# Layer norms taken by token halves, with ScalarE centring and scaling three of four chunks, in a fused two-layer transformer kernel

## The reference, cut to what matters

```python
def layer_norm(x, g, b):
    xf = x.astype(jnp.float32)
    mu = xf.mean(-1, keepdims=True)
    var = jnp.square(xf - mu).mean(-1, keepdims=True)
    return ((xf - mu) * lax.rsqrt(var + LN_EPS) * g.astype(jnp.float32) + b.astype(jnp.float32)).astype(x.dtype)

def swiglu(x, w_in, w_out):
    g, u = jnp.split(x @ w_in, 2, axis=-1)
    return (jax.nn.silu(g) * u) @ w_out

# first_block
y = hybrid_mixer(x, ...)
x = layer_norm(ALPHA * x + y, ln_g[l, 0], ln_b[l, 0])
y = mem_cross_attention(x, mem, w_q_mem[l], w_kv_mem[l], w_o_mem[l])
x = layer_norm(ALPHA * x + y, ln_g[l, 1], ln_b[l, 1])
y = swiglu(x, w_ffn_in[l], w_ffn_out[l])
x = layer_norm(ALPHA * x + y, ln_g[l, 2], ln_b[l, 2])

# second_block
hn = rmsnorm(x, norm_g)
proj = jnp.einsum('bsd,dc->bsc', hn, w_in)
```

## Time and profile before

| | |
|---|---|
| median of 3 runs | 2252.07 us (2250.58 to 2252.34) |
| the profiled execution | 2250.64 us, span 2248.8 us |
| TensorE busy | 2231.8 us, 99% of the span |
| VectorE, ScalarE, GpSimd busy | 58%, 46%, 8% |
| mean granted TensorE clock | 0.998 |
| chain that ended last | TensorE 96%, VectorE 2%, GpSimd 1% |
| weights and x read | 418 MB, 187 GB/s over the span |

### The profile page before, as it was taken

One profiled execution on the slowest core, in us unless ns is written; L12 is line 12 of the kernel. 1 busy time (PEld: TensorE's weight loads), 2 busy tenths in 40 slices (PEclk: granted clock), 3 DMA queues, 4 the chain that ended last, 5 costly groups with the idle time before them and its releaser, 6 DMA issues.

```text
span 2248.8 us, 29509 instructions
## 1 busy us (share of the span) xinstructions
PE 2231.8 (99%) x10256; PEld 1849.3 (82%) x10256; DVE 1307.9 (58%) x1571; ACT 1038.8 (46%) x1239; POOL 173.0 (8%) x175
## 2 busy tenths in 40 slices
PE   9999999999999999999999999999999999999999
PEld 8888888888888788888888888877888888888887
DVE  5555655566667854454445545566666656645674
ACT  4444445545444444433444344435445454445643
POOL 1000000001203210000000000003000000200020
PEclk9999999999999999999999999999999999999999
DMA  7755654556755365656655565555566665765554
GB/s 234 227 174 164 185 159 159 189 163 213 263 177 198 123 230 181 197 190 193 192 189 187 187 197 186 192 172 159 161 194 197 195 194 171 218 186 174 168 188 167
DMA packets 216454, 421.29 MB, mean 187 GB/s; under 512 B 15240, under 2 KB 19376, under 8 KB 214448
## 3 DMA queue, kind: packets, MB, share of 16 engines
q1 hardware_dynamic: 212928, 401.79, 56.5%
q0 software_dynamic: 3168, 17.82, 2.4%
q10 hardware_dynamic: 272, 0.52, 0.1%
HBM read 417.97 MB, written 2.11 MB: 187 GB/s over the span
## 4 chain that ended last, share of the span: by engine, by line
PE 96%; DVE 2%; POOL 1%; DMA 0%; ACT 0%; issue 0%; ACTq 0%; SPq 0%; DVEq 0%
PE b_ps L571 90%; PE b_ps L599 1%; PE b_ps L616 1%; PE b_ps L668 1%; DVE b_w_lo L1479 1%; PE b_ps L683 1%; POOL b_x_res L499 1%; DVE b_x_res L1630 0%; DVE b_x_res L1639 0%; PE b_ps L677 0%; PE b_ps L759 0%; PE b_ps L736 0%; POOL b_x_res L510 0%; POOL b_x_res L505 0%; PE b_ps L684 0%; DMA b_gate_a<-in_x 0%
## 5 line engine op out<-in xcount | busy, mean ns | idle before, releaser
L1479 DVE TENSOR_TENSOR b_w_lo<-b_stage,b_w_hi 128x1024 fp32r<-128x1024 f32 (+1 forms) x762 | 935.2, 1246 | 618.1 <-ACT b_w_hi L1065 615.3
L1065 ACT ACTIVATE b_w_hi<-b_stage 128x1024 fp32r<-128x1024 f32 (+1 forms) x762 | 794.5, 1054 | 685.2 <-PE b_ps L571 656.7
L571 PE MATMUL b_ps<-b_w_hi,b_x_hi 128*128 128x512 f32 (+1 forms) x2364 | 938.5, 397 | 0.7 <-DVE b_w_lo L1479 0.5
L571 PE MATMUL b_ps<-b_w_hi,b_x_lo 128*128 128x512 f32 (+1 forms) x2364 | 921.0, 390 | 0.0
L571 PE MATMUL b_ps<-b_w_lo,b_x_hi 128*128 128x512 f32 (+1 forms) x2364 | 919.4, 389 | 0.0
L571 PEld LDWEIGHTS b_ps<-b_w_hi,b_x_lo 128*128 128x128 f32 x2364 | 444.5, 188 | 93.6
L571 PEld LDWEIGHTS b_ps<-b_w_hi,b_x_hi 128*128 128x128 f32 x2364 | 445.0, 188 | 92.2 <-issue 3.2
L571 PEld LDWEIGHTS b_ps<-b_w_lo,b_x_hi 128*128 128x128 f32 x2364 | 445.2, 188 | 87.6
L571 PE MATMUL b_ps<-b_w_hi,b_ff_h 128*128 128x512 f32 x352 | 137.3, 390 | 0.0
L571 PE MATMUL b_ps<-b_w_hi,b_ff_l 128*128 128x512 f32 x352 | 137.0, 389 | 0.0
L571 PE MATMUL b_ps<-b_w_lo,b_ff_h 128*128 128x512 f32 x352 | 136.9, 389 | 0.0
(11 more groups left out here) (294 smaller groups left out, 1462.3 us busy)
## 6 DMA issues: line engine op xcount, KB each, us to landing
b_stage<-in_w_in SPq DMA_DIRECT2D x335, 512.0 KB, 4.2
b_stage<-in_w_ffn_in SPq DMA_DIRECT2D x176, 512.0 KB, 4.5
b_stage<-in_w_ffn_out SPq DMA_DIRECT2D x88, 512.0 KB, 4.1
b_stage<-in_w_out SPq DMA_DIRECT2D x64, 512.0 KB, 4.0
b_stage<-in_w_up SPq DMA_DIRECT2D x24, 512.0 KB, 4.1
b_stage<-in_w_o_dsa SPq DMA_DIRECT2D x16, 512.0 KB, 4.7
b_stage<-in_w_o_moba SPq DMA_DIRECT2D x16, 512.0 KB, 4.3
b_stage<-in_w_kv_mem SPq DMA_DIRECT2D x16, 512.0 KB, 3.5
```

Of the source, the lines that this page charges most:

```text
L571: ins = mm(ps[:, ACC + r, 0:n], x[:, kt + t, rows], w[:, slot, t, 0:n], start=first and t == 0 and k == 0, stop=last and t == GK - 1 and k ...
L1065: act.activation(w_hi[:, slot, :, 0:n], stage[:, slot, :, 0:n], ACT.Copy)\
L1479: dve.tensor_tensor(w_lo[:, slot, :, 0:n], stage[:, slot, :, 0:n], w_hi[:, slot, :, 0:n].bitcast(F32), ALU.subtract).then_inc(sem("lo_done ...
```

## The change

In norms 1 and 2 (`feed_normed`, `norm_and_feed`) the work goes by token halves. Norm 0 keeps its split of work.

- TensorE: in the last block before each of the two norms the last two groups run for half 0, then for half 1 (`two_groups`, `rows_last`). The first two groups after the norm do the same. Batches 0 and 1 are turned for half 0, then two half groups, then batches 0 and 1 for half 1, directly followed by batches 2 and 3, which go to two other PSUM banks (`SC`, `PT`), then the two other half groups. Fillers go from 19 + 15 to 3 + 6 + 3 + 4.
- VectorE does residual, statistics, aggregation, centring of all 512 columns of chunk one, root and scaling for half 0, then the residual of half 1 and the low parts of half 0, then the same for half 1. It also computes `shift` = -mean x rstd. Chunk two is no longer its work.
- ScalarE does (x - mean) x rstd for chunks two to four as x x rstd + shift. Batches 2 and 3 are turned from that; weight and bias of the norm, which then lie along partitions, are applied as it reads PSUM (`ln_gc`, `ln_bc`, result in `nat`), and high and low parts are taken from `nat`.
- GpSimd only multiplies by the weight and adds the bias (`weigh`), in chunks three, four, then two.
- Four more loads of 128 x 16 single elements bring `ln_gc` and `ln_bc`; for norm 2 GpSimd multiplies them once by `g_col`.
- In norm 0 GpSimd's multiply and add alternate by half, each waiting for the one before.

The core of the diff:

```diff
-LN_FILL = (19, 15)
+LN_FILL = (3, 6, 3, 4, 5)
@@ GpSimd
+            for m in (1, 2):
+                load(ln_gc[:, m - 1, :], a["ln_g"][m, :].rearrange("(t p) -> p t", p=P), "small2",
+                     allow_slow_non_contiguous=True)
+                load(ln_bc[:, m - 1, :], a["ln_b"][m, :].rearrange("(t p) -> p t", p=P), "small2",
+                     allow_slow_non_contiguous=True)
...
+                    for n in (2, 3):
+                        for r in range(R):
+                            pool.wait_ge(sem("scaled"), 5 * m - 5 + (1, 3, 4, 5)[2 * (n - 2) + r])
+                            ins = weigh(n, r)
+                        ins.then_inc(sem("late_chunk"), 1)
+                    pool.wait_ge(sem("tp_done"), c.at(f"turned{m}"))
                     for r in range(R):
...
+                        ins = weigh(1, r)
@@ TensorE
+            def two_groups(kt, first, last, hi, lo, ready=None):
+
+                slot = c.value("g") % SLOTS
+                for r in range(R):
+                    for i in range(2):
+                        if ready:
+                            ready(r, i)
+                        if r == 0:
+                            pe.wait_ge(sem("lo_done"), c.next("lo_done"))
+                        half_group((slot + i) % SLOTS, r, kt + i * GK, first and i == 0, last and i == 1, hi, lo)
+                c.next("g", 2)
...
+                def rows_ready(r, i):
+                    if i == 0:
+                        keep_warm(LN_FILL[2 * r])
+                        for t in range(2):
+                            pe.wait_ge(sem("chunk"), 4 * m + 2 * r + t)
+                            turn_rows(t, r).then_inc(sem("tp_done"), 1)
+                        c.next("tp_free", 2)
+                        if r == 1:
+                            pe.wait_ge(sem("scaled"), 5 * m - 3)
+                            for t in (2, 3):
+                                for row in range(R):
+                                    ins = turn_rows(t, row)
+                                ins.then_inc(sem("tp_done"), 1)
+                            c.next("tp_free", 2)
+                        keep_warm(LN_FILL[2 * r + 1])
+                    pe.wait_ge(sem("tp_free"), fed + 2 * r + i + 1)
+                two_groups(0, True, False, x_hi, x_lo, ready=rows_ready)
+                for j in range(2, KT // GK):
+                    pe.wait_ge(sem("tp_free"), fed + 4 + j - 1)
+                    group(j * GK, False, j == KT // GK - 1, x_hi, x_lo)
+                    if j + 2 < KT // GK:
+                        if j % 2 == 0:
+                            pe.wait_ge(sem("late_chunk"), 3 * m - 1 + j // 2)
+                        feed_batch(x_res, j + 2)
@@ ScalarE
+                for r in range(R):
+                    root(sd[:, r:r + 1])
+                    if r == 1:
+                        scaled(1, 0)
+                        act.wait_ge(sem("norm_ready"), 1 + 2 * m)
+                        scaled(1, 1).then_inc(sem("scaled"), 1)
+                    else:
+                        act.wait_ge(sem("norm_ready"), 2 * m)
+                    for t in range(2):
+                        hi_rows(t, r, scale)
+                    if r == 0:
+                        split()
+                        scaled(2, 0).then_inc(sem("scaled"), 1)
@@ VectorE
+            def norm_and_feed(m, i, alpha, vecs, scale=None):
+
+                residual(i, alpha, True, (0,))
+                rows_normed(0, vecs)
+                residual(i, alpha, False, (1,))
+                for t in range(2):
+                    lo_rows(t, 0, scale)
+                statistics(i, 1)
+                rows_normed(1, vecs)
+                for t in range(2):
+                    lo_rows(t, 1, scale)
+                split()
+                for t in (2, 3):
+                    scaled_batch(t)
+                split()
+                for j in range(KT // GK):
+                    if 0 < j < KT // GK - 1:
+                        split()
+                    c.next("w_used")
+                    if 1 < j < KT // GK - 2:
+                        lo_batch(x_hi[:, 2 * j + 4:2 * j + 6, :], x_lo[:, 2 * j + 4:2 * j + 6, :], j + 2, scale)
```

More of the change, by code:

```diff
@@ L260, in two_blocks, with bank_of, columns @@
         mem_out = [ps[:, bank, 0:S] for bank in (PT, OT, TP, TP + 1)]
+        def bank_of(t, normed):
+            return (SC, PT)[t - 2] if normed and t in (2, 3) else TP + t % 2
+        def columns(t):
+            return [slice(2 * t + k, 2 * t + k + 1) for k in range(2)]
         ext = nc.dram_tensor("rel_ext", [H_B2, 2 * S - 1], F32).ap()
@@ L583, in weights @@
                         before(j)
+                    if rows_last and j == groups - 2:
+                        two_groups(j * GK, j == 0, True, hi, lo)
+                        break
                     if isinstance(c.value("g"), int) and c.value("g") == 0:
@@ L1126, in after @@
                     if hook:
                         hook(j)
-                weights(hook=after)
             def root(x):
@@ L1534, in lo_part, with lo_rows @@
                     lo_batch(hi(t), lo(t), t)
[L1536 to L1546 removed]
+            def lo_rows(t, r, scale=None):
+                dve.wait_ge(sem("hi_t"), c.next("hi_t"))
+                rows = slice(r * P, (r + 1) * P)
+                hi, lo = x_hi[:, 2 * t:2 * t + 2, rows], x_lo[:, 2 * t:2 * t + 2, rows]
+                src = ps[:, TP + t, :].rearrange("p (k s) -> p k s", k=2)[:, :, rows]
+                if scale is None:
+                    ins = dve.tensor_tensor(lo, src, hi.bitcast(F32), ALU.subtract)
+                else:
+                    for k in range(2):
+                        ins = dve.scalar_tensor_tensor(
+                            out=lo[:, k, :], in0=src[:, k, :], scalar=scale[:, 2 * t + k:2 * t + k + 1],
+                            in1=hi[:, k, :].bitcast(F32), op0=ALU.mult, op1=ALU.subtract)
+                ins.then_inc(sem("tp_free"), 1)
+                c.next("tp_done")
+                c.next("tp_free")
             def inverse_root(x, n, mean, eps):
@@ L1610, in gated_at, with residual @@
                     c.next(f"tile_out{r}")
-            def residual(i, alpha, stat):
+            def residual(i, alpha, stat, rows=range(R)):
                 cols = ds(i * NB, NB)
-                for r in range(R):
+                for r in rows:
                     tile_done(r)
@@ L1660, in norm_chunk @@
                 centre(cols)
-                rescale(cols)
+                rescale(cols).then_inc(sem("chunk"), 1)
             for name in TOKENS["dve"]:
```

253 lines of the change are left out of this document (164 added, 89 removed).

## The result

| | before | changed |
|---|---|---|
| median | 2251.47 us (2250.58 to 2252.34, 8 runs) | 2256.61 us (2255.95 to 2259.46, 8 runs) |
| ratio | | 1.0025 (95%: 1.0015 to 1.0035) |
| profiled execution | 2250.64 us, span 2248.8 | 2256.58 us, span 2255.0 |
| mean granted clock | 0.998 | 1.000 |

The forecast was 2245.7 us with a range of 2240 to 2251. The changed kernel took 5.1 us more than the one before, not 5 to 6 less.

What follows compares the result with a forecast made beforehand. TensorE was taken to bound the kernel, losing 23.3 us in norms 1 and 2. Gains of 10.1 us, less 1.0 for the clock and 2.7 for column loads, gave -6.4 from 2252.07: 2245.7 us, range 2240 to 2251.

Steps and rivals of the forecast that it cites:

- At nothing: Items priced at zero, such as GpSimd's order in norm 0, later loads and weight forms: together plus or minus 0.7 us.
- rival (a): The forecast itself holds for the whole kernel: some 2243 to 2247.5 us, chance 0.48.
- rival (d): Column loads at 594 to 603 us delay weights without cover: slower, 2257 us or more, chance 0.06.
- The first token half: After the last block before each norm, TensorE stands 2.1 us in norm 1 and 0.8 in norm 2.
- Fillers and low parts: After the first half's transposes, pair gap, fillers and waiting for low parts: 1.0 us in norm 1, 1.35 in norm 2.
- The second token half: VectorE's chain, its centring delayed by GpSimd, costs TensorE 2.3 us in each norm, bounds 1.05 and 3.5.
- The fifth group: Waits behind ScalarE's and VectorE's queues: 1.0 us in norm 1 (0 to 1.2), 2.3 in norm 2 (0.8 to 2.9).
- The clock: TensorE granted 1.2 GHz for stretches after the norms' gaps: 1.0 us for both norms, between 0 and 3.4.
- The column loads: Four small loads at 587 us slow weight traffic where TensorE is uncovered: 2.7 us added, bounds 0 and 4.
- late_chunk: Sign in the norms: if it holds the sixth or seventh batch over 1 us, the sum is wrong.
- GpSimd's chunk three: In norm 1, 2 x 3.2 us of GpSimd work after 782 against TensorE's need near 790: hidden, by about 1 us.

Runs made afterwards that it cites:

- e12_no_fillers: Changed kernel at old tile addresses, column loads 110 us later, batches before splits, GpSimd's chunk three later, without filler transposes: 2239.49 us, 0.9949 of the kernel before.
- e7: Changed kernel at old tile addresses, ScalarE and VectorE taking the next batch before the next weight split in normed blocks: 2243.36 us, 0.9963 of the kernel before.

## Why the prediction was wrong, point by point

**The step that failed.** It is the list "At nothing", with its plus or minus 0.7 us. It went through the moved work and left out the diff's line on `align`. I read it as padding that keeps the tiles in place, and never worked out whether it did. It cost 12.3 us: the 2040 matmuls with a late stationary operand, unchanged and waiting for nobody, went from 227 to 233 ns each. Without it the kernel takes 2244.27, inside what rival (a) forecast (2243 to 2247.5) and 1.4 below the number. With it the sum, 2245.7 + 12.3 = 2258.0, is close to the measured 2256.6. The range could not hold such a term, since no bound in it was about the rate of undisturbed matmuls. My one slower rival (d) named a place that was not at fault.

**The first token half: right.** TensorE stood 1.72 us in norm 1 (774.16 to 775.88; predicted 2.1) and 0.74 in norm 2 (0.8). Fillers and low parts took 0.99 and 1.42 us over the transposes (1.0 and 1.35).

**The second token half: right in size, at another instruction.** From the half groups' end to the next group TensorE took 3.51 us in norm 1 (780.23 to 783.74) and 3.70 in norm 2; less twelve transposes of 0.11 us, 2.2 and 2.4 were lost (predicted 2.3 each). I had put GpSimd's delay on the centring. GpSimd's multiply did start 0.27 us into the centring, but the centring took its usual 0.74 us and the multiply grew, to 1.62 us from the 1.28 that it takes alone (785.68). The two rescalings behind it bore the delay:

```profile
778.60 0.74 DVE L1775 SCALAR_TENSOR_TENSOR b_x_res<-b_x_res,b_mv,b_vec_a 128x512 f32<-128x512 f32 x1
...
779.58 2.60 DVE L1806 SCALAR_TENSOR_TENSOR b_x_res<-b_x_res,b_rstd,b_vec_b 128x256 f32<-128x256 f32 x2
```

```profile
778.87 1.62 POOL L523 TENSOR_TENSOR b_x_res<-b_x_res,b_vec_a 128x512 f32<-128x512 f32 x1 [76.34 <-ACT b_x_res L1228]
780.57 1.32 POOL L525 TENSOR_TENSOR b_x_res<-b_x_res,b_vec_b 128x512 f32<-128x512 f32 x1
```

Taken one by one, the first rescaling ends at 780.78, 0.3 us after the multiply (780.50), and the second at 782.18, 0.3 us after the add (781.90). So VectorE waited until each of GpSimd's two instructions had ended. It lost 1.73 us and not the sum of both, since the multiply had run for 0.7 us when the first rescaling came. The Trainium skill (SBUF — State Buffer, "SBUF: two separate sides") has the two lock each other out for a whole instruction. These rows agree, and so do and the earlier trace rows, which I misread in the prediction: taken singly, VectorE's first centring beside GpSimd (775.47) ends at 777.24, 0.55 us after GpSimd's multiply (775.40, 1.29 us). The 1.5 us that I took for GpSimd's own time is a mean of that 1.29 and of 1.72, which holds a wait.

**The fifth group: mis-sized in norm 1.** 1.7 us lost there (predicted 1.0) and 1.9 in norm 2 (2.3). VectorE's two splits in front of the low part took 3.98 us beside GpSimd, not 2.4. The fourth group's wait for w_lo, 0.4 us in each norm, was not foreseen. Norm 1 lost 7.3 us where I had 6.4, and norm 2 7.2 where I had 6.75.

**The clock: too much for the median.** I booked 1.0 us for low stretches in the norms. The profiled execution had none, and its mean granted clock went from 0.998 to 1.000: the gain of the norms holds the 1.7 us and more that the earlier trace rows showed. But three of the eight executions had 0.998 or 0.999 and took 2258.22 to 2259.46 us, where the other five lie between 2255.95 and 2256.65. That the clock never fell, as the text of e12_no_fillers says, holds for the profiled execution only.

**The column loads: right.** Predicted 2.7, between 1.8 and 2.9 by three runs (the step in the changed kernel's own trace is 3.3); TensorE's waits at 603 and 608 us sum to 2.3, in the 2 to 3 that I gave as the sign.

**The others.** `late_chunk` held nobody in the changed kernel. GpSimd's chunk three was "hidden, by about 1 us", and so it was: ready at 788.3, transposed at 789.3. Chunk four had no term in the prediction. It was ready at 797.9 for transposes at 798.0, and in time only because the fifth group waited, as e7 showed.

## What to carry to other kernels

Price the line of a diff that allocates, as every other. A tile of a few bytes can move all tiles behind it, and a matmul that nobody touched becomes slower with no wait to show for it; compare the mean duration of the same instruction before and after. Where two waits stand in a row on different engines, take both away at once: by the traces one edit alone gained 1.2 us up to the seventh group of the two norms and the other 1.3, and both on top of the moved loads 4.4 (3.9 by the medians, 2241.57 to 2237.66).

## What the hardware showed that I had not expected

Matmuls of 512 columns in this kernel follow each other at 227 ns when the stationary and the streamed operand start a multiple of 256 bytes apart in a partition (the kernel before, the realigned one, all tiles +32, late tiles -256 and -512), and at 232 to 234 when they are 32, 64, 96 or 128 bytes off it. That is 2 to 3%, and with every weight matmul off it cost 57 us of 2251. The absolute starts did not matter: with all tiles 32 bytes higher the ratio was 1.0001 (0.9992 to 1.0011). The duration of a weight load stayed between 187 and 189 ns in every case, and matmuls of 336 columns kept their 154 ns with the operands 96 bytes off.

Where VectorE's and GpSimd's instructions on `x_res` met, the one that came second waited for the first to end: VectorE's rescalings of 256 columns ended 0.3 us after GpSimd's instruction, its centrings of 512 columns 0.55 us after it, and GpSimd's multiply behind a centring grew from 1.28 to 1.62 us.

Four loads of 128 x 16 single elements, 32 KB in all, held the transfers at 110 GB/s for 5 us and at 156 GB/s for 6 us at the other place, where the kernel before moves 217 and 409.
